# Eight gate columns of a token mixer: from a padded weight tile to fp32 products on 32-column parts of the array

## What is computed

```python
def token_mix(h, w_in, ...):
    proj = h @ w_in                       # w_in: 1024 x 3592
    sb_qkv, gdn_qkv, gdn_z, gdn_a, gdn_b, sc_bch = jnp.split(proj, [...], axis=-1)
    ...                                   # stick-breaking attention on sb_qkv
    gdn_qkv = jax.nn.silu(causal_dwconv(gdn_qkv, gdn_conv_w))
    ...
    beta = jax.nn.sigmoid(gdn_b)          # 4 heads
    log_decay = -jnp.exp(gdn_a_log) * jax.nn.softplus(gdn_a + gdn_dt_bias)   # 4 heads
    o_gdn = gated_delta_rule_chunked(g_q, g_k, g_v, log_decay, beta)
    ...
    return mixed @ w_out
```

## Time and profile before

| | |
|---|---|
| median of 3 executions | 3321.43 us (3320.43 to 3321.92) |
| profiled execution, first to last instruction | 3318.5 us |
| profiled execution, its whole device time | not recorded beside the span |
| TensorE busy | 3270.9 us, 99% of the span |
| VectorE (DVE) / ScalarE (ACT) / GpSimd (POOL) busy | 43% / 41% / 45% |
| read from HBM | 280.72 MB, 86 GB/s over the span |
| mean granted TensorE clock | 0.999 |

### The profile page before, as it was taken

How to read it: one execution, slowest core, us unless ns; L and a number is a source line. 1 busy time by engine, 2 the same in 40 slices (tenths; PEclk the granted TensorE clock), 3 DMA queues, 4 the chain that set the end, 5 groups by cost and what they waited for, 6 DMA issues and landing times. The chain is left out here.

```text
span 3318.5 us, 45351 instructions
## 1 busy us (share of the span) xinstructions
PE 3270.9 (99%) x16390; PEld 2728.1 (82%) x16390; DVE 1438.7 (43%) x2419; ACT 1370.2 (41%) x2201; POOL 1477.2 (45%) x1109
## 2 busy tenths in 40 slices
PE   9999999999999999999999999999999999999999
PEld 7888887888888888888788888888888888888777
DVE  3421475652204722136676222274465266235643
ACT  4322455542224522234655222265355255445553
POOL 4554443144543555444323554445454454354423
PEclk9999999999999999999999999999999999999999
DMA  5422222022322222222211332233221221232111
GB/s 176 146 95 95 89 77 69 26 89 98 98 95 83 94 97 95 95 93 86 70 33 64 104 99 95 89 134 99 77 70 64 77 79 67 76 132 81 58 57 64
DMA packets 78200, 289.14 MB, mean 87 GB/s; under 512 B 8672, under 2 KB 8800, under 8 KB 76896
## 3 DMA queue, kind: packets, MB, share of 16 engines
q1 hardware_dynamic: 76176, 275.77, 25.3%
q10 hardware_dynamic: 1872, 11.27, 0.9%
HBM read 280.72 MB, written 6.29 MB: 86 GB/s over the span
## 5 line engine op out<-in xcount | busy, mean ns | idle before, releaser
L614 POOL TENSOR_TENSOR w_lo<-raw,w_hi 128x512 fp32r<-128x512 f32 x1026 | 1381.1, 1369 | 1581.4 <-ACT w_hi L683 1581.2
L2127 PE MATMUL ps<-x_hi,w_hi 128*128 128x512 f32 x2536 | 1011.2, 399 | 1.9 <-DVE b_q L1857 1.0
L2129 PE MATMUL ps<-x_hi,w_lo 128*128 128x512 f32 x2536 | 988.2, 390 | 0.0
L2128 PE MATMUL ps<-x_lo,w_hi 128*128 128x512 f32 x2536 | 987.5, 389 | 0.0
L683 ACT ACTIVATE w_hi<-raw 128x1024 fp32r<-128x1024 f32 x514 | 541.6, 1055 | 968.3 <-PE ps L2129 494.1
L2127 PEld LDWEIGHTS ps<-x_hi,w_hi 128*128 128x128 f32 x2536 | 476.5, 188 | 110.2 <-issue 12.6
L2128 PEld LDWEIGHTS ps<-x_lo,w_hi 128*128 128x128 f32 x2536 | 476.5, 188 | 104.2 <-issue 8.4
L2129 PEld LDWEIGHTS ps<-x_hi,w_lo 128*128 128x128 f32 x2536 | 476.1, 188 | 99.7
L1417 DVE TENSOR_TENSOR T<-T,ps 128x512 f32<-128x512 f32 x66 | 45.4, 688 | 470.5 <-PE ps L2129 464.2
L634 POOL TENSOR_TENSOR square_parts<-T,square_parts 128x512 fp32r<-128x512 f32 (+1 forms) x71 | 87.9, 1240 | 238.5 <-ACT square_parts L1060 238.5
L2263 PE MATMUL ps<-h_hi,w_hi 128*128 128x512 f32 (+1 forms) x440 | 153.3, 348 | 0.0
(11 more groups left out here) (376 smaller groups left out, 5118.9 us busy)
## 6 DMA issues: line engine op xcount, KB each, us to landing
raw<-in_weights SPq DMA_DIRECT2D x514, 512.0 KB, 3.3
Y<-in_x_t SPq DMA_DIRECT2D x4, 512.0 KB, 6.6
mem_split<-norm_hi ACTq DMA_DIRECT2D x2, 1024.0 KB, 3.9
mem_split<-norm_lo ACTq DMA_DIRECT2D x2, 1024.0 KB, 5.9
mem_hi<-mem_split ACTq DMA_DIRECT2D x2, 1024.0 KB, 7.4
mem_lo<-mem_split ACTq DMA_DIRECT2D x2, 1024.0 KB, 9.9
out_t<-Y SPq DMA_DIRECT2D x8, 256.0 KB, 2.0
mem<-in_mem_t SPq DMA_DIRECT2D x1, 1024.0 KB, 13.5
```

The costliest lines, as they stand in the source:

```text
L614: ins = pool.tensor_tensor(g.wl[:, k, part], g.raw[:, k, part], g.wh[:, k, part], ALU.subtract)
L2127: mm(out, wh[:, c], xh[:, kc, :], start=kc == 0, stop=False)
L2128: mm(out, wh[:, c], xl[:, kc, :], start=False, stop=False)
L2129: ins = mm(out, wl[:, c], xh[:, kc, :], start=False, stop=kc == DC - 1)
```

## The change

The gates leave the weight stream. Their weights come as a small array of their own, `ab_w`: for each of the 8 chunks 128 x 32, of which 8 columns are used. ACT loads it (128 KB a layer) as the `middle` action of the norm before the mixer, when the last output unit of the feed-forward is done, because it lies over the last KB of h_lo. After `first_tiles`, which now takes tiles 1, 2 and 3, TensorE makes 8 plain fp32 products from Y itself: chunk kc goes to the 32-column part kc % 4 of the array and so to 32 partitions of bank 6, two chunks summed in each part. DVE copies the whole bank (128 x 512), and the four transposes behind tile 4 become products with a 128 x 8 selection matrix that sums the four parts. The input units of a mixer go from 29 to 28, and `tile` is called for v = 4 to 28. Tiles 1 to 3 move to banks 0 to 2. Counts that went by 29 a layer go by 28.

```diff
-U_FFN_IN, U_FFN_OUT, U_MIX, U_MIX_OUT, U_PLE = 2 * FFC, FFC, MIX_TILES + 1, DC, DC + 2
+U_FFN_IN, U_FFN_OUT, U_MIX, U_MIX_OUT, U_PLE = 2 * FFC, FFC, MIX_TILES, DC, DC + 2
...
+        g.ABW = over("ab_weights", (P, DC, 32), F32, 87)
...
 def mix_bank(v):
-    return v % 4 if v < SB_START else 3 + (v - SB_START + 1) % 3
+    return v - 1 if v < SB_START else 3 + (v - SB_START + 1) % 3
+
+
+def mix_base(m):
+
+    return BASE[f"mix{m}"] - 1
...
+        def ab_weights():
+
+            act.wait_ge(s.unit_done, v0 + FFC)
+            act.dma_start(g.ABW[:, :, :], T["ab_w"][:, c // 2, :, :]).then_inc(s.ab_landed, 16)
+
-        norm(n, eps_ffn, [w0 + 12, w0 + 13, w0 + 14], None, arena if c % 2 else None)
+        norm(n, eps_ffn, [w0 + 12, w0 + 13, w0 + 14], None, arena if c % 2 else ab_weights)
...
-        for w in range(29):
+        for w in range(1, 29):
...
+            if w == SB_START:
+                dve.wait_ge(s.ab_mm, m + 1)
+                v.tensor_copy(g.AB[:, :], ps[:, 6, :]).then_inc(s.ab_evac, 1)
             dve.wait_ge(s.unit_done, u0 + w + 1)
             src = ps[:, mix_bank(w), :]
-            if w == 0:
-                v.tensor_copy(g.AB[0:8, :], src[0:8, :]).then_inc(s.proj_evac, 1)
-            elif V_CONV <= w < V_SC:
+            if V_CONV <= w < V_SC:
...
-        u0 = BASE[f"mix{m}"]
-
-        first_tiles(mixer_norm(m), u0, [ps[:, b, :] for b in range(3)])
-        for v in range(3, 29):
+        u0 = mix_base(m)
+
+        first_tiles(mixer_norm(m), u0 + 1, [ps[:, mix_bank(v), :] for v in range(1, 4)])
+        pe.wait_ge(s.x_done, by_half(4 * m, 1, DC - 1))
+        pe.wait_ge(s.ab_landed, 16 * (m + 1))
+        for kc in range(DC):
+            at = 32 * (kc % 4)
+            ins = mm(ps[at:at + 32, 6, :], g.ABW[:, kc, :], g.Y[:, kc, :], start=kc < 4, stop=kc >= 4,
+                     skip_group_check=True)
+        ins.then_inc(s.ab_mm, 1)
+        for v in range(SB_START, 29):
...
             if v == SB_START:

-                pe.wait_ge(s.proj_evac, 29 * m + SB_START)
+                pe.wait_ge(s.proj_evac, 28 * m + SB_START - 1)
+                pe.wait_ge(s.ab_evac, m + 1)
+                select = g.vec[:, VEC["select"][0]:VEC["select"][0] + 8]
                 for n in range(NT):
-                    ins = nc.tensor.transpose(ps[:, 7, 8 * n:8 * n + 8], g.AB[0:8, n * P:(n + 1) * P],
-                                              ident[0:8, 0:8])
+                    ins = mm(ps[:, 7, 8 * n:8 * n + 8], g.AB[:, n * P:(n + 1) * P], select, start=True, stop=True)
                 ins.then_inc(s.ab_t, 1)
...
+def gate_weights(w):
+
+    out = np.zeros((P, DEPTH, DC, 32), np.float32)
+    out[:, :, :, 0:8] = w[:, :, 2816:2824].reshape(DEPTH, DC, P, 8).transpose(2, 0, 1, 3)
+    return out
...
+           "select": (np.arange(P)[:, None] % 32 == np.arange(8)).astype(np.float32)
```

More of the change, by code:

```diff
@@ L61 @@
                   ("dt_bias", 8), ("ple_b", 16), ("norm_g", 16), ("mem_g", 16), ("mem_q", 2), ("mem_k", 2),
-                  ("qn_a", 3), ("kn_a", 3), ("qn_b", 1), ("kn_b", 1)):
+                  ("qn_a", 3), ("kn_a", 3), ("qn_b", 1), ("kn_b", 1), ("select", 8)):
     VEC[_name] = (_at, _n)
@@ L213, in build @@
             mixsrc_done mixhi_done mixlo_done qksq_done ss_done ssr_done qkn_done
-            ab_t gates_in gates_out g_done gcol_mm gcol_done ug_done gb_mm eg_done kd_in so_done egc_done
+            ab_landed ab_mm ab_evac ab_t gates_in gates_out g_done gcol_mm gcol_done ug_done gb_mm eg_done kd_in so_done egc_done
             xzero_done ea_done dec_in dec_out kk_mm m_done kt_done kd_done vt_done vb_done c_done xmat_done xcopy_done ymat_done turn_done dcopy_done
@@ L639, in pool_program @@
         for n in range(NT):
-            low_many(at, BASE[f"mix{m}"] + V_DECAY + 1 + n + RING + 1)
-            at = BASE[f"mix{m}"] + V_DECAY + 1 + n + RING + 1
+            low_many(at, mix_base(m) + V_DECAY + 1 + n + RING + 1)
+            at = mix_base(m) + V_DECAY + 1 + n + RING + 1
             pool.wait_ge(s.eg_done, 4 * m + n + 1)
@@ L868, in mixer @@
     def mixer(m):
-        u0 = BASE[f"mix{m}"]
-        for v in range(29):
+        u0 = mix_base(m)
+        for v in range(1, 29):
             if v == 28:
@@ L945, in mixer @@
                 for t in range(0, 8) if v == 16 else range(8, 12):
-                    act.wait_ge(s.proj_evac, 29 * m + V_CONV + t + 1)
+                    act.wait_ge(s.proj_evac, 28 * m + V_CONV + t)
                     fn(g.CV[:, t, :], g.CV[:, t, :], ACT.Silu).then_inc(s.cvs_done, 1)
@@ L971, in mixer @@
             if 10 <= j < 14:
-                act.wait_ge(s.proj_evac, 29 * m + V_SC + 5 + (j - 10) // 2)
+                act.wait_ge(s.proj_evac, 28 * m + V_SC + 4 + (j - 10) // 2)
                 mix_hi(m, j - 6, 1 + j // 2, g.PR[:, 7 + j // 2, :])
@@ L975, in mixer @@
                 k = j // 3 - 5
-                act.wait_ge(s.proj_evac, 29 * m + V_Z + k + 1)
+                act.wait_ge(s.proj_evac, 28 * m + V_Z + k)
                 fn(g.PR[:, k, :], g.PR[:, k, :], ACT.Silu).then_inc(s.z_done, 1)
@@ L1507, in short_conv @@
                 return
-            dve.wait_ge(s.proj_evac, 29 * m + V_SC + k)
+            dve.wait_ge(s.proj_evac, 28 * m + V_SC + k - 1)
             v.tensor_tensor(c, c, src, ALU.mult).then_inc(s.proj_evac, 1)
-            dve.wait_ge(s.proj_evac, 29 * m + V_SC + k + 1)
+            dve.wait_ge(s.proj_evac, 28 * m + V_SC + k)
             link(v.tensor_scalar(h, c, tap(0), None, ALU.mult))
@@ L2372, in mixer @@
     def mixer(m):
-        u0 = BASE[f"mix{m}"]
-        first_tiles(mixer_norm(m), u0, [ps[:, b, :] for b in range(3)])
-        for v in range(3, 29):
+        u0 = mix_base(m)
+        first_tiles(mixer_norm(m), u0 + 1, [ps[:, mix_bank(v), :] for v in range(1, 4)])
[7 more added lines that the diff above has]
+        for v in range(SB_START, 29):
             bank = mix_bank(v)
-            last = [w for w in range(v) if mix_bank(w) == bank]
+            last = [w for w in range(1, v) if mix_bank(w) == bank]
             if last:
-                pe.wait_ge(s.proj_evac, 29 * m + last[-1] + 1)
+                pe.wait_ge(s.proj_evac, 28 * m + last[-1])
             h = sb_head(v, SB_SUM)
@@ L2384, in mixer @@
             if v == SB_START:
-                pe.wait_ge(s.proj_evac, 29 * m + SB_START)
+                pe.wait_ge(s.proj_evac, 28 * m + SB_START - 1)
+                pe.wait_ge(s.ab_evac, m + 1)
+                select = g.vec[:, VEC["select"][0]:VEC["select"][0] + 8]
                 for n in range(NT):
-                    ins = nc.tensor.transpose(ps[:, 7, 8 * n:8 * n + 8], g.AB[0:8, n * P:(n + 1) * P],
-                                              ident[0:8, 0:8])
+                    ins = mm(ps[:, 7, 8 * n:8 * n + 8], g.AB[:, n * P:(n + 1) * P], select, start=True, stop=True)
                 ins.then_inc(s.ab_t, 1)
             if v == V_VT:
-                pe.wait_ge(s.proj_evac, 29 * m + V_CONV)
+                pe.wait_ge(s.proj_evac, 28 * m + V_CONV - 1)
                 pe.wait_ge(s.gates_in, m + 1)
@@ L2474, in mixer @@
                 ins.then_inc(s.vt_done, 1)
-        pe.wait_ge(s.proj_evac, 29 * m + 29)
+        pe.wait_ge(s.proj_evac, 28 * m + 28)
         def join_y(j):
@@ L2923, in weight_stream @@
                 w = x["mix_w_in"][l]
-                ab = np.zeros((D, P), w.dtype)
-                ab[:, 0:8] = w[:, 2816:2824]
                 gate, c, h = (w[:, 2824 + 256 * k:3080 + 256 * k].reshape(D, 2, P) for k in range(3))
@@ L2928, in weight_stream @@
                 order = np.concatenate([w[:, 0:2304], sc, w[:, 2304:2816]], axis=1)
-                parts += [weight_tiles(ab), weight_tiles(order), weight_tiles(x["mix_w_out"][l])]
+                parts += [weight_tiles(order), weight_tiles(x["mix_w_out"][l])]
             else:
@@ L2972, in vector_table @@
            "qn_a": columns(x["qn_a_2"]), "kn_a": columns(x["kn_a_2"]), "qn_b": columns(x["qn_b_2"]),
-           "kn_b": columns(x["kn_b_2"])}
+           "kn_b": columns(x["kn_b_2"]), "select": (np.arange(P)[:, None] % 32 == np.arange(8)).astype(np.float32)}
     return np.concatenate([sep[n] for n in VEC], axis=1)
@@ L3040 @@
         "mem_t": feature_major(x["mem_2"][0]),
+        "ab_w": gate_weights(x["mix_w_in"]),
         "vecs": vector_table(x),
```

## The result

Before: 3321.39 us, median of 4 runs (3320.43 to 3321.92). After: 3335.48 us, median of 4 (3335.08 to 3335.72). The ratio is 1.0044, interval [1.0032, 1.0055]: slower by 14.1 us, where 5.7 us of gain were forecast.

The account below looks back on a forecast made before the run. TensorE, busy 99% of the span, was taken as the bound. Per layer 5.44 - 2.07 - 0.54 = 2.83 us, 5.7 us over two layers, gave 3321.4 - 5.7 = 3315.7 us, range 3312.8 to 3320.4.

Parts of the forecast that it names:

- What bounds the kernel: Whole kernel: TensorE, busy 99% of the span; time comes off only where it gets less to do or idles less.
- The tile that goes, -5.44: Mixer's tiles: one whole tile of 24 products disappears, saving 5.44 us a layer.
- the net of 2.83 a layer: Each mixer: 5.44 saved, less 2.07 for gate products and 0.54 for selection; 5.7 us over two layers.
- The gate products, 2.07: Block behind the split tiles: four array parts work at once, 1.72 us plus 0.35 of edges a layer.
- The two outer edges of the sum: Around the gate products: 0.09 us ahead and 0.11 behind, of 0.35 us of edges in all.
- The ratio of three parts: Gate products: the skill's 2.38 times for three column tiles, giving an estimated 2.17 us in place of 1.72.
- Strict order: Rival on the gate products: matmuls in strict FIFO, 4.22 us a layer, 3320.0 us in all; 13%.
- The selection, 0.88: Behind tile 4: eight records of 0.11 us replace transposes of 0.34 us, adding 0.54 us a layer.
- What moves, at 0: Weight load, DVE copies, weight units and banks: all covered by slack, 0 us; ACT's issue takes 0.37 us.
- parts in series: Slower rival on the gate products: no overlap, 7.23 us a block, 3326.1 us; 4%, another 2% with late weights.
- the cheap case: Rival on gate products and selection: edges gone, selection at no extra cost, 3.72 us gained a layer, 3314.0 us; 16%.
- What would show it wrong: Profile after: a new TensorE wait at tile 4 or 5, or a span falling less than the two blocks explain.

Follow-up runs that it names:

- e14: e5 with one more iteration of ACT's loop over the first feed-forward written out ahead of it, moving ACT's code: 3315.32 us, ratio 0.9983.
- e15: e5 with three more iterations of ACT's first feed-forward loop written out than e14's one plus e5's own, moving ACT's code: 3315.03 us, ratio 0.9983.
- e13: e5 with the load of the gate weights issued by SP instead of by ACT in the norm: 3315.49 us, ratio 0.9983.
- e8: e5 with all eight gate products on one 32-column part of the array, so nothing can overlap: 3326.93 us, ratio 1.0015.
- e2: The kernel before, with 32 unused bytes put behind `vec` and nothing else changed: 3340.47 us, ratio 1.0056.
- e3: The kernel before, with 32 bytes ahead of the arena alone, constants in place: 3337.18 us, ratio 1.0049.
- e5: The changed kernel with every old address, its eight selection columns in an own tensor behind h_lo with an own load: 3316.9 us, ratio 0.9984.
- e7: The kernel before, with the arena alone 64 bytes on, constants in place: 3326.04 us, ratio 1.0014.
- e12: The kernel before, with 96 bytes between w_lo and all that follows: 3388.95 us, one run.
- e6: The kernel before, with every tensor 32 bytes on, all distances between tensors kept: 3321.1 us, ratio 0.9998.
- e9: The kernel before, with 32 bytes between raw and w_hi: 3322.01 us, ratio 1.0.
- e10: The kernel before, with 32 bytes between w_lo and all that follows: 3386.03 us, one run.
- e4: The kernel before, with the constants 32 bytes on and the arena 64 bytes on: 3328.54 us, ratio 1.0022.
- e1: The changed kernel, with all that follows `vec` moved on to the next multiple of 64 bytes: 3323.01 us, ratio 1.0005.

## Why the prediction was wrong

**What bounds the kernel:** right. TensorE is busy 99% before and after, and nearly all that was lost was lost in its own products.

**The tile that goes, -5.44, and the net of 2.83 a layer:** right, within 0.1 us a layer. Two like records frame the edit: the last split product (392.59 before, 397.56 after) and the first scores of the attention behind the selection (404.05 and 406.08). The lag of the changed kernel behind the kernel before falls from 4.96 to 2.03 us between them in the first mixer, and from 8.16 to 5.23 in the second: 2.93 us in both. With the old places and the code moved the whole gain is 5.9 and 6.2 us (e14, e15), and 5.7 in e13, where 5.7 was summed.

**The gate products, 2.07:** right in mechanism, four parts at once, and in size. From first record to next tile it is 1.85 us, 0.13 over the 1.72. The two outer edges of the sum come on top: 0.09 ahead (the last split product starts at 397.56 and takes 0.12, the block starts at 397.77) and 0.11 behind (399.62 to 399.96 in place of 0.23). Together 2.05. The ratio of three parts in the Trainium skill (TensorE: Matmul & The Clock Gate, Measured speedup vs the span model) would have given, as an estimate, 2.17 without edges; the trace lies under that, and e8 has the ratio of four parts at 6.99/1.85 = 3.8. Strict order falls: four records start in one window of 0.1 us, and 4.22 us was its price.

**The selection, 0.88:** measured 0.88. The edge of 0.09 ahead of the transposes shrank to 0.01 (the last tile product starts at 404.96 and takes 0.23, the selection starts at 405.20); that is the 0.1 by which 2.93 exceeds 2.83.

**What moves, at 0: here the prediction failed**, in two places.

First and by far the larger: the part listed each queue and each wait, and took as untouched whatever was not mentioned, the addresses of all tensors behind `vec` among it. The eight columns of the selection matrix stand in the quoted diff; that they lengthen a tensor in the middle of the layout was not priced. In its place: e2 puts the cost of that shift alone at 19.4 us, of which the arena is 16.1 (e3) and the constants' place 3.3. From e13 (-5.7) to after (+14.1) there are 19.8 us; 19.4 of shift leave 0.4 for ACT's late issue, where the records read 1.6. The two agree only within what totals of these runs resolve, some 3 us each way. Of the arena's 16.1 us, 14.1 are counted product by product above; the rest was not followed.

Second: the issue of the weight load, put at 0.37 us in an idle slot of 1.02, outgrew the slot in the first layer: it took 3.42 us with a packet of code inside it. TensorE lost 1.6 us by it, in after and in e5, 0.97 and 0.90 of it as idle time. No row of the trace before showed such a wait on ACT; the bound of 0.37 us was that of an undisturbed issue.

**The rivals.** None of them was it. The one on the slower side, parts in series, was the wrong mechanism, and its 3326.1 us is well under the 3335.48 measured. All rivals concerned the block that was edited; the loss came in each of the four feed-forwards' outputs and through the second block, where nothing had been edited. The range ended at 3320.4 for the same reason. (Its lower end, the cheap case less one stretch of the clock, comes to 3314.0 - 1.7 = 3312.3 and not 3312.8; nothing hangs on it.)

**What would show it wrong** was named rightly in one of its two forms: "a span that falls by less than the two blocks explain". The blocks came out as summed and the span did not fall.

## What to carry to other kernels

Whoever adds a column to a table in SBUF moves every tensor behind it. Read the layout as part of the change, keep the distance of streamed operands to the weights (put new small tensors at the end, as e5 does), and compare the mean record of the products that were not edited before anything else: 6 ns on 389 was nearly the whole story here. A version with this in order, e14 or e15, runs the same change 5.9 or 6.2 us under the kernel before.

When an issue or a short instruction is costed into an idle slot, ask what it costs if a packet of code falls beside it; moving the code by one loop iteration took the long issue away here (3.35 us in e5, 0.39 in e14), and a later edit that moves code may bring it back.

## What the runs showed of the hardware that was not expected

- Reduced float32 products of 512 columns start 226.7 ns apart when streamed operand and weights lie at the distances of the kernel before, 233.4 when the streamed tensor is 32 bytes further (e3), 228.0 to 229.8 at 64 (e7), and at 96, for the x products, 232.1 to 234.2 (e12). At 256 columns the order turns round: 120 before, 117 in the changed kernel, 116.5 at 64 bytes. Shifting all tensors together costs nothing (e6), and raw's place costs nothing (e9). That the reads of the streamed operand and of the next weights meet each other fits all of this; no run separates it from other readers of w_hi and w_lo, so it stays an inference. e10 to e12 are one run each. Distances beyond 96 bytes were not tried.
- Products that take a constant as stationary operand are touched as well, though their streamed operand did not move: 228.1 to 231.3 ns on ones_r between e7 and e4. They are 0.4 us of the 3.0 that the constants' place costs there; most of the rest is in products on x, many of them beside one on ones_r. Why those are longer was not followed.
- Plain fp32 products on four 32-column parts run side by side: 16 records in 1.85 us, against 6.99 on one part.
- The issue of the gate weights' transfer on ACT took 0.34 to 0.39 us in the second layer of after, e1, e5 and e8 and in both layers of e14 and e15, and 2.46 to 3.42 us in the first layer of after, e1, e5 and e8, where a code packet fell inside it. Why SP's issue in e13 took 1.07 us was not followed.
